# A depthwise convolution shared between three engines: samples' taps to GpSimd and a VectorE sum, fewer TensorE taps, another order of the last pooling group

## The reference

```python
proj = h @ p["w_in_ab"][i]
xa = proj[..., :D_A]
a = proj[..., D_A:D_A + D_B]
gt = proj[..., D_A + D_B:]
ya, pb = multi_scale_pool(xa, pool_bufs[i], start_pos, p["pool_w"][i], p["pool_scale"][i])
glu = a * jax.nn.sigmoid(gt)
c, cb = causal_dwconv(glu, conv_bufs[i], p["conv_w"][i], p["conv_b"][i])
yb = jax.nn.silu(layernorm(c, p["conv_norm_g"][i], p["conv_norm_b"][i]))
x = x + jnp.concatenate([ya, yb], axis=-1) @ p["w_out_ab"][i]
```

## Time and profile before

| | us |
|---|---|
| median of 3 runs | 1206.99 |
| lowest and highest | 1206.85, 1207.07 |
| the profiled execution: its time | 1207.7 |
| its span in the trace | 1205.9 |
| TensorE busy | 1186.9 (98%) |
| VectorE busy | 741.7 (62%) |
| GpSimd busy | 623.7 (52%) |
| ScalarE busy | 508.6 (42%) |

### The profile page before, as it was taken

The page is one execution under the profiler, slowest core; times in us unless marked ns, Lnnn a source line. Parts: engine busy times, 40 slices in busy tenths (PEclk is TensorE's granted clock), DMA queues, the critical chain, the costliest instruction groups (busy, mean ns, idle before and its releaser), DMA issues.

```text
span 1205.9 us, 21702 instructions
## 1 busy us (share of the span) xinstructions
PE 1186.9 (98%) x8636; PEld 1156.7 (96%) x8636; DVE 741.7 (62%) x1499; ACT 508.6 (42%) x880; POOL 623.7 (52%) x632
## 2 busy tenths in 40 slices
PE   7999999999999999999999999999999999999997
PEld 7887799999999999999999999999999999999997
DVE  5999555567945688454521754345687557865554
ACT  6333455445434454343521532344443344433442
POOL 4643435436963469543455323443489344884433
PEclk9999999999999999999999999999999999999999
DMA  6310124321332213422322221322214222242212
GB/s 241 112 36 27 44 67 139 105 70 35 106 140 70 70 35 106 141 74 67 123 88 82 64 84 62 122 71 88 70 36 157 88 70 70 70 141 71 66 54 79
DMA packets 33652, 103.74 MB, mean 86 GB/s; under 512 B 4880, under 2 KB 6928, under 8 KB 33552
## 3 DMA queue, kind: packets, MB, share of 16 engines
q1 hardware_dynamic: 29488, 98.92, 25.0%
q10 hardware_dynamic: 4080, 3.69, 1.0%
HBM read 98.29 MB, written 4.79 MB: 85 GB/s over the span
## 4 chain that ended last, share of the span: by engine, by line
PE 89%; DVE 4%; ACT 2%; DMA 1%; issue 1%; POOL 1%; ACTq 0%; POOLq 0%; SPq 0%; DVEq 0%
PE psum L408 67%; PE psum L606 13%; PE psum L504 3%; PE psum L736 3%; DVE psum L1846 1%; DVE psum L1734 1%; PE psum L448 1%; POOL w_lo L1340 1%; DVE squares_sum L2002 1%; DMA w_raw<-in_w_down 1%; PE psum L686 1%; DVE block_lo L1734 1%; PE psum L456 0%; ACT psum L1061 0%; DVE arena L1971 0%
## 5 line engine op out<-in xcount | busy, mean ns | idle before, releaser
L408 PE MATMUL psum<-x_hi,w_hi 128*128 128x288 f32 x1856 | 402.0, 298 | 6.7 <-ACT w_hi L782 6.7
L408 PE MATMUL psum<-x_hi,w_lo 128*128 128x288 f32 x1856 | 398.6, 296 | 1.1 <-POOL w_lo L1260 1.1
L408 PE MATMUL psum<-x_lo,w_hi 128*128 128x288 f32 x1856 | 398.2, 296 | 0.0
L1260 POOL TENSOR_TENSOR w_lo<-w_raw,w_hi 128x1024 fp32r<-128x1024 f32 (+2 forms) x102 | 226.8, 2228 | 275.3 <-ACT w_hi L782 275.3
L408 PEld LDWEIGHTS psum<-x_hi,w_hi 128*128 128x128 f32 x1856 | 300.0, 189 | 8.8 <-ACT w_hi L782 6.6
L408 PEld LDWEIGHTS psum<-x_hi,w_lo 128*128 128x128 f32 x1856 | 299.9, 189 | 1.5 <-POOL w_lo L1260 1.5
L408 PEld LDWEIGHTS psum<-x_lo,w_hi 128*128 128x128 f32 x1856 | 300.0, 189 | 0.0
L1846 DVE SCALAR_TENSOR_TENSOR psum<-arena,params,psum 128x608 f32<-128x608 f32 x176 | 150.6, 856 | 88.5 <-ACT psum L1061 84.1
L1260 POOL TENSOR_TENSOR w_lo<-arena,w_hi 128x1024 fp32r<-128x1024 f32 (+1 forms) x49 | 114.6, 2338 | 119.9 <-ACT w_hi L782 119.9
L782 ACT ACTIVATE w_hi<-w_raw 128x1024 fp32r<-128x1024 f32 (+2 forms) x102 | 98.5, 970 | 88.5 <-PE psum L408 79.6
L606 PE MATMUL psum<-block_hi,w_hi 128*128 128x288 f32 x448 | 133.4, 298 | 0.2 <-POOL w_lo L1340 0.2
(11 more groups left out here) (208 smaller groups left out, 1619.2 us busy)
## 6 DMA issues: line engine op xcount, KB each, us to landing
w_raw<-in_w_up SPq DMA_DIRECT2D x44, 512.0 KB, 3.4
arena<-in_w_up SPq DMA_DIRECT2D x44, 512.0 KB, 3.4
w_raw<-in_w_down SPq DMA_DIRECT2D x16, 512.0 KB, 3.6
arena<-in_w_down SPq DMA_DIRECT2D x16, 512.0 KB, 3.6
w_raw<-in_w_in_c SPq DMA_DIRECT2D x16, 512.0 KB, 3.3
w_raw<-in_w_in_ab SPq DMA_DIRECT2D x12, 512.0 KB, 3.6
w_raw<-in_w_out_ab SPq DMA_DIRECT2D x16, 256.0 KB, 2.6
w_raw<-in_w_out_c SPq DMA_DIRECT2D x8, 512.0 KB, 3.4
```

The source lines that it names most:

```text
L408: last = nc.tensor.matmul(PS[:, 2 * (q % 2 if slot is None else slot) + half, 0:HALF], w[q][:, k * P:(k + 1) * P], r[:, r_at, half * HALF: ...
L1260: nc.gpsimd.tensor_tensor(w_lo[slot][:, 0:nk * P], raws[RAW_SLOT[RAW[u]]][:, 0:nk * P], w_hi[slot][:, 0:nk * P].bitcast(F32), ALU.subtract ...
```

## The change

Four things change, all within layer 0's convolution.

1. Samples. GpSimd computes all 31 x 64 = 1984 products of a tile in one instruction (`sample_products`), which writes into space of the later high and low parts; VectorE sums each 31 with one `tensor_reduce` (`sum_samples`) and adds the bias in one 64-column instruction. One buffer serves all tiles, so the products of tile c wait for the sum of tile c - 1.
2. Taps. TensorE does 6, 7, 7 and 10 taps of the tiles, VectorE 25, 24, 24 and 21, for the prompt alone, in two chains in two PSUM banks that `merge` adds up.
3. Feature sums. GpSimd adds the finished tiles 0, 1 and 2 (`conv_sum`), and `conv_mean` multiplies that sum and tile 3 only.
4. `pool_map(3)` stands in the middle of taps(3) instead of behind it.

```diff
-    PE_TAPS = 10
-    V_TAPS = TAPS - PE_TAPS
+    PE_TAPS = (6, 7, 7, 10)
+    V_TAPS = [TAPS - n for n in PE_TAPS]
...
+        tap_products = mem[:, (KD + KH) * T:(KD + KH) * T + SM * TAPS].rearrange("p (s t k) -> p s t k", s=NS, t=DS)
+        conv_sum = mem[:, KH * T:KH * T + T]
...
-                for n in range(PE_TAPS):
-                    k = V_TAPS + n
+                for n in range(PE_TAPS[c]):
+                    if middle is not None and n == PE_TAPS[c] // 2:
+                        middle()
+                    k = V_TAPS[c] + n
...
-            def conv_mean(c):
-
-                for half in range(2):
-                    last = nc.tensor.matmul(PS[:, M0 + half, 0:HALF], ones[:, :],
...
+            def conv_mean():
+
+                for src in (conv_sum, conv_o[:, KH - 1, :]):
+                    for half in range(2):
+                        last = nc.tensor.matmul(PS[:, M0 + half, 0:HALF], ones[:, :], src[:, half * HALF:(half + 1) * HALF],
+                                                start=(src is conv_sum), stop=(src is not conv_sum))
+                last.then_inc(mean_mm, 1)
...
-            conv_taps(3)
-            pool_map(3, 1, U_IN0 + 12)
+            conv_taps(3, lambda: pool_map(3, 1, U_IN0 + 12))
...
+            def sample_products(c):
+
+                pool.wait_ge(glu_ready, 2 * c + 2)
+                if c:
+                    pool.wait_ge(taps_summed, c)
...
+                nc.gpsimd.tensor_tensor(tap_products,
+                                        bass.AP(first.tensor, first.offset, [first.ap[0], [CB + DS, NS], [1, DS], [1, TAPS]]),
+                                        bass.AP(weights.tensor, weights.offset, [weights.ap[0], [0, NS], [0, DS], [KH, TAPS]]),
+                                        ALU.mult).then_inc(tap_products_ready, 1)
+
             for u in range(1, N_IN0):
                 split_n(u + 3)
+                if u in (2, 5, 8, 11):
+                    sample_products(u // 3)
...
+                    nc.gpsimd.tensor_tensor(conv_sum, conv_o[:, 0, :], conv_o[:, 1, :], ALU.add).then_inc(conv_summed, 1)
...
+            nc.gpsimd.tensor_tensor(conv_sum, conv_sum, conv_o[:, 2, :], ALU.add).then_inc(conv_summed, 1)
...
+            def sum_samples(c):
+                dve.wait_ge(tap_products_ready, c + 1)
+                nc.vector.tensor_reduce(smp(conv_o[:, c, PR:T]), tap_products, AX.X, ALU.add).then_inc(taps_summed, 1)
+
+            def merge(c):
+
+                dve.wait_ge(conv_step, sum(V_TAPS[:c + 1]))
+                nc.vector.tensor_tensor(conv_o[:, c, 0:PR], PS[:, (S1, M1)[V_TAPS[c] % 2], 0:PR], conv_o[:, c, 0:PR],
+                                        ALU.add).then_inc(taps_merged, 1)
+                dve.wait_ge(taps_summed, c + 1)
+                nc.vector.tensor_scalar(conv_o[:, c, PR:T], conv_o[:, c, PR:T], pcol("conv_b", c), None, ALU.add)\
+                    .then_inc(conv_samples, 1)
...
+            make_glu(3)
+            conv(2, 20, V_TAPS[2])
+            sum_samples(2)
+            merge(2)
+            conv(3, 0, 3)
             combine(2)
-            conv(3, 9, 15)
+            conv(3, 3, 8)
             evacuate(11)
-            conv(3, 15, V_TAPS)
-            combine_samples(3)
+            conv(3, 8, V_TAPS[3])
+            sum_samples(3)
+            merge(3)
             combine(3)
```

More of the change, by code:

```diff
@@ L555, in _ @@
             pe.wait_ge(conv_samples, KH)
-            for c in range(KH):
-                last = conv_mean(c)
-            last.then_inc(mean_mm, 1)
+            pe.wait_ge(conv_summed, KH - 2)
+            conv_mean()
             ya_unit(1)
@@ L1557, in make_glu @@
                                         smp(g_t[:, PR:T]), ALU.mult).then_inc(glu_ready, 1)
[L1559 removed]
             def conv(c, first, end):
                 dve.wait_ge(glu_ready, 2 * c + 2)
[L1564 to L1573 removed]
+                if c and first == 0:
+                    dve.wait_ge(taps_merged, c)
@@ L1574, in step @@
+                for k in range(first, end):
+                    acc, win, w = PS[:, (S1, M1)[k % 2], 0:PR], glu[:, c, k:k + PR], pcol("conv_w", k * KH + c)
+                    if k == 0:
+                        ins = nc.vector.tensor_scalar(acc, win, w, pcol("conv_b", c), ALU.mult, ALU.add)
+                    elif k == 1:
                         ins = nc.vector.tensor_scalar(acc, win, w, None, ALU.mult)
                     else:
-                        ins = nc.vector.tensor_scalar(acc, win, w, pcol("conv_b", c), ALU.mult, ALU.add)
+                        dve.wait_ge(conv_step, sum(V_TAPS[:c]) + k - 1)
+                        ins = nc.vector.scalar_tensor_tensor(out=conv_o[:, c, 0:PR] if k == V_TAPS[c] - 1 else acc,
+                                                             in0=win, scalar=w, in1=acc, op0=ALU.mult, op1=ALU.add)
@@ L1577, in step @@
                     ins.then_inc(conv_step, 1)
-                    steps_made[0] += 1
-                    behind[chain] = steps_made[0]
-                new = smp(conv_o[:, c, PR:T])
-                samples = lambda k: smp(glu[:, c, CB + PR:GL], CB + DS)[:, :, k:k + DS]
-                for k in range(first, end):
-                    last = k == V_TAPS - 1
-                    step("p", conv_o[:, c, 0:PR], k, PS[:, S1, 0:PR], glu[:, c, k:k + PR], last)
-                    step("s", new, k, smp(PS[:, M1, 0:SM]), samples(k), last)
-                    if k % 2:
-                        step("r", None, V_TAPS + k // 2, smp(PS[:, M1, SM:2 * SM]), samples(V_TAPS + k // 2))
```

77 lines of the change are left out of this document (33 added, 44 removed).

## The result

| | before | changed |
|---|---|---|
| median, us (18 runs each) | 1207.27 | 1209.41 |
| lowest and highest, us | 1206.41, 1208.42 | 1207.58, 1214.71 |
| ratio of the medians, with its 95% interval | | 1.0022 [1.0014, 1.0031] |
| the profiled execution: time, span | 1207.7, 1205.9 | 1208.98, 1207.2 |
| TensorE's granted clock over the span | 0.999 | 0.995 |

The changed kernel is 2.1 us slower. I had forecast 1.4 us less, so the prediction had the sign wrong; the time lies within its range.

What follows compares the result with a forecast made beforehand. TensorE was taken to bound the kernel, VectorE narrowly keeping up. Of 11.5 us shed, 10.3 come back as waits behind the held bias; -1.4 us from 1207.0 gives 1205.6 us, range 1195.3 to 1211.0 for 8 in 10.

Steps and rivals of the forecast that it cites:

- What TensorE sheds: TensorE's queue: ten taps fewer 8.6 us, half the feature sums 1.9, map(3)'s place up to 1.0; in all 11.5.
- VectorE's prices: VectorE in the convolution: prompt tap 0.66 us, sample step 0.19, reduction 2.14, merge 0.6, bias about 0.15.
- I take 4.3: GpSimd's product of 1984 columns: 4.3 us at the pace of additions, between bounds of 3.1 and 5.5.
- the forecast's 1.5, 3.0, 2.4 and 3.0: TensorE's forecast waits in us: at unit 7, unit 10, taps(3) and map(3), in that order.
- For 5.5 us I had also worked out the sum: With products of 5.5 us alone, tile 0's bias comes ahead of them; the mean ends at 137.1, no change.
- The upper-bound rival of 1211.0: Held VectorE queue with products of 5.5 us and sum of 2.67: mean ends at 141.0, 1211.0 us; chance 0.25.
- each us of product and sum costs about four: Every tile pays for longer sum and products; from about 7.4 us for both, slower by more than 0.2%.
- The mechanism of the held bias: VectorE's SBUF-to-SBUF bias stands until GpSimd's running product ends: held some 3.7 us, possible for tiles 0, 1 and 2.
- the rival that it isn't held: VectorE's bias runs free beside GpSimd and only glu collides: mean ends at 125.5, 1195.5 us; chance 0.27.
- 1.9 us lost in glu(1): VectorE loses 1.9 us in glu(1) between GpSimd's window sums, after evacuating unit 4.
- short products: GpSimd's products at 3.1 us, or a sum of 1.2: mean ends at 132.4, 1202.4 us; chance 0.13.
- 6.4 us and 1210.7: By the skill's rule for reads with a step over 8 bytes, products take about 6.4 us: 1210.7 us.

Runs made afterwards that it cites:

- e10: e5 with the feature sums over all four tiles instead of the sum of three and the last: 1197.73 us.
- e1: The changed kernel with the products of tile c + 1 waiting for the bias addition of tile c instead of its sum: 1198.24 us.
- e7: e1 with ten taps on TensorE for every tile, as before the change: 1203.93 us.
- p1: The kernel before, with only map(3) moved between the fifth and sixth tap of tile 3: 1206.08 us.
- e3: The changed kernel with GpSimd's multiplication reading 31 neighbouring columns (wrong weights) instead of every fourth: 1205.98 us.
- e8: The changed kernel with unused multiplications filling TensorE's waits ahead of unit 10, tile 3's taps and map(3): 1206.76 us.
- e2: The changed kernel with the reduction writing to a free PSUM bank and the bias addition reading it there: 1198.55 us.
- e5: e1 with the convolution's weights laid down tile by tile, so GpSimd reads a tile's 31 side by side: 1195.25 us.
- e6: e1 with map(3) behind tile 3's ten taps again instead of between the fifth and sixth: 1198.37 us.

## Why the prediction was wrong

- **What TensorE sheds** was right. e10 measures the feature sums at 1.93 us for 1.9. Putting the ten taps back onto e1 costs 6.0 (e7), and that is the 8.6 less e1's wait of 2.0 at map(3), which they fill, and some 0.6 us of rest. map(3)'s new place was put at "up to 1.0"; p1 shows 0.3 in the trace.
- **VectorE's prices** were right: 0.66 us a tap (47.67 to 53.60 is 9 taps), the reduction 2.20 (2.12 from its start to the next) for my 2.14, the bias 0.24 (0.18 to the next) for 0.15 to 0.2.
- **The step that failed is a term of the sum: "I take 4.3" for the product.** It takes 5.6, near my upper bound of 5.5. The reason for taking 4.3, "the form being that of the additions", left out the step of four columns, which I had before me and set down under a rival. e3 puts 1.4 us on it, and with the step gone my schedule comes true: 0.9, 2.4, 2.0 and 2.8 us of waits for the forecast's 1.5, 3.0, 2.4 and 3.0, and 1206.0 for 1205.6, the time less firmly than the waits, as said above.
- **For 5.5 us I had also worked out the sum**: tile 0's bias ahead of the products, and the feature sums at 137.1, "no change". That is what happened up to the clock: no wait at unit 7, the bias of tile 0 0.4 us, the waits 4.7, 1.5 and 2.9, and without the half clock a stretch 0.15 us longer than before (e8). The upper-bound rival of 1211.0 needed the sum at 2.67 us as well, and did not come; that 1209.4 lies near it owes 1.9 us to the clock, of which it knew nothing. Its rule that each us of product and sum costs about four, slower by over 0.2% from 7.4 us for both, contradicts the "no change" for 5.5 (7.6 for both) and was wrong: at 7.8 us for both the kernel without the half clock is 0.15 us over before, since tile 0's bias no longer pays.
- **The clock was in no term.** The 4.7 us wait is followed by half clock, which hides (unit 10's 2.3 us come off the wait at tile 3's taps), and the one at map(3) is followed by another spell, which does not hide: 1.9 us. That is all of the difference between "no change" and +2.1. Of the 3.5 us between the forecast's -1.4 and the measured +2.1 the product's length makes 1.6 and the clock 1.9: the first takes the gain away, the second gives the sign.
- **The mechanism of the held bias** was right, and the rival that it isn't held falls (the rows, e1, e2). What the hold costs a tile was the product's length less 0.6, as said; with 5.6 that is 5.0 instead of 3.7. The rival's own time, 1195.5 us with products of 4.3, is what e5 measures with the bias free and products of 4.2: 1195.25.
- **glu.** I reckoned 1.9 us lost in glu(1); it was 1.2, and glu(2), of which I said nothing, lost some 3.5 us beside two splits. In e5 glu(2) still loses over 2 us, and TensorE doesn't wait: the slack of VectorE covers it there, while in the changed kernel it lies on the chain to the wait at unit 10.
- **A bound that doesn't follow.** For short products I took 3.1 us from 710 columns in 1.37 us. At that pace, 1.93 ns a column, 1984 columns take 3.8 us. The runs show nothing under 4.1.
- **The wait at map(3)** had the size that I gave, 2.9 for 3.0, by another releaser. ScalarE's reading of map(2)'s result, behind its part of the window sums and a table load of 1.28 us, ended at 125.84; GpSimd's window sums, which I had named, at 125.75. The two paths are 0.1 us apart, so by the rows a cure for one alone would have done next to nothing; no run tries it.

The Trainium skill (GPSIMD Engine Reference, Performance pitfalls for Q7 kernels) has the direction of the step's cost: a read with a step over 8 bytes costs half as much again, a rule for kernels of one's own on GpSimd. Here a built-in multiplication has the step in one of its two inputs, and the measurement says 5.59 / 4.18, a third more. By that rule I had 6.4 us and 1210.7 for the whole, on the right side and 1.3 us over the measurement, though without the clock in it. On the port the Trainium skill (SBUF — State Buffer, Who interferes with whom) agrees in all three cases that the runs show: the SBUF-to-SBUF bias is held (5.2 us), the one that reads PSUM isn't (0.28 us), and the reduction never was (2.21 us with GpSimd busy or idle).

## What to carry to other kernels

When an instruction's end releases a long one on GpSimd, look at what VectorE does next: a short instruction from SBUF to SBUF there cost nearly the whole of the long one. Letting the long one wait for the short (e1) or giving the short one its input in PSUM (e2) was worth 11 us here, 1.9 of them by way of the clock.

What a held engine costs is the slack that isn't there. The same two holds of 5 us cost 0.3 us with ten taps a tile on TensorE and 11 us with 6, 7, 7 and 10, so count a shift of work together with the stalls of the engine that receives it.

Where the sum shows new waits on TensorE, price a spell at half clock behind them too, from rows at that clock, and look in every trace whether there is one before comparing two lengths (e6). And where the operand of a long instruction is small and fixed, lay it down in the order of reading.

## What the runs showed of the hardware that I had not expected

- TensorE ran at half clock (0.50) behind waits of 4.7 and 3.3 us, and in the changed kernel also behind one of 2.9 us, after the taps that followed a wait of 1.5; in e6 behind waits of 0.8 and 1.1. In the profiled execution of e3 it kept full clock behind waits of 2.4 and 2.8 us, in e1 behind one of 2.0. So the length of the last wait alone doesn't tell. Multiplications without use in the waits kept it at 1.00 and saved 1.9 us.
- In runs of the changed kernel with a mean clock of 0.993 instead of 0.995 the time was 1213 to 1214.7 us; the kernel before stayed between 1206.4 and 1208.4 in the runs beside them. That more such spells make the difference is likely, but I have no trace of one of those runs.
- A GpSimd multiplication of 1984 columns took (medians) 4.18 us with both inputs in neighbouring columns and 5.59 us with one input at a step of four.
- A VectorE reduction of 1984 columns to 64 took 2.20 us, 1.1 ns for each column read, whether it wrote SBUF or PSUM (2.23).
